# Another order of splits, copies and remainders around the last head pair of a hybrid encoder, with two token tiles' output products interleaved

## The reference

```python
def _dilated_attention_mixer(h, w_in, w_out):
    proj = h @ w_in                      # q, k, v of three dilation groups, and a gate
    for g, (window, dil) in enumerate(((128, 1), (512, 4), (2048, 16))):
        o, l = _dilated_group(q, k, v, window, dil, slopes)    # softmax attention, log denominators
    wts = jax.nn.softmax(jnp.stack(lses, axis=-1), axis=-1)
    o = jnp.einsum('bshg,bshgd->bshd', wts, jnp.stack(outs, axis=3))
    y = o.reshape(bsz, s, A_WIDTH) * jax.nn.silu(gate)
    return y @ w_out

x = _layer_norm(DEEPNORM_ALPHA * x + gate * y, ln_g, ln_b)
```

## Time and profile before

| | us |
|---|---|
| median of 3 runs | 1970.03 (1969.86 to 1972.2) |
| profiled execution | 1972.37 |
| its span, first to last instruction | 1970.6 |
| mean granted clock of TensorE | 0.993 |

### The profile page before, as it was taken

The page is one execution under the profiler, slowest core; times in us unless marked ns, Lnnn a source line. Parts: engine busy times, 40 slices in busy tenths (PEclk is TensorE's granted clock), DMA queues, the critical chain, the costliest instruction groups (busy, mean ns, idle before and its releaser), DMA issues.

```text
span 1970.6 us, 33735 instructions
## 1 busy us (share of the span) xinstructions
PE 1917.3 (97%) x12422; PEld 1532.3 (78%) x12422; DVE 1301.3 (66%) x2634; ACT 1047.3 (53%) x2578; POOL 1266.0 (64%) x841
## 2 busy tenths in 40 slices
PE   7999999999999999999998999899999999999998
PEld 4788887888888878888877777687787777777887
DVE  6547566475664756646666767887788697587553
ACT  5455555555555555554562354864765765774320
POOL 0566776967769677686762825565666575586572
PEclk8999999999999999999999999999999999999999
DMA  9112222322223222132245416455455455366531
GB/s 293 53 60 70 79 86 62 97 69 76 81 71 94 64 78 86 63 96 71 79 146 184 145 54 150 135 148 161 135 171 150 138 168 146 133 191 231 180 119 43
DMA packets 117987, 229.45 MB, mean 116 GB/s; under 512 B 23104, under 2 KB 56256, under 8 KB 117824
## 3 DMA queue, kind: packets, MB, share of 16 engines
q1 hardware_dynamic: 117824, 227.29, 37.2%
HBM read 199.39 MB, written 27.86 MB: 115 GB/s over the span
## 4 chain that ended last, share of the span: by engine, by line
PE 81%; DVE 8%; ACT 3%; issue 3%; POOL 2%; SPq 2%; DMA 1%; DVEq 0%; ACTq 0%; POOLq 0%
PE pp L693 18%; PE pp_s L2581 15%; PE pp L696 9%; PE po L693 7%; PE po L696 4%; PE tp L775 3%; PE po L845 3%; PE sp_ L763 3%; DVE stage_s L3261 2%; PE yo_p L2785 2%; PE pp_s L2785 2%; PE st_p L2598 1%; PE st_p L2785 1%; PE fill L2785 1%; DVE vv L3182 1%
## 5 line engine op out<-in xcount | busy, mean ns | idle before, releaser
L693 PE MATMUL pp<-h_forms_hi,w_f 128*128 128x512 f32 x788 | 317.0, 402 | 3.2 <-ACT w_f L1049 3.2
L693 PE MATMUL pp<-h_forms_lo,w_f 128*128 128x512 f32 x788 | 308.2, 391 | 0.0
L579 POOL TENSOR_TENSOR w_f<-w_raw,w_f 128x512 fp32r<-128x512 f32 x154 | 197.1, 1300 | 145.0 <-ACT w_f L1049 145.0
L2581 PE MATMUL pp_s<-h_hi,w_hi_s 128*128 128x512 f32 x624 | 269.6, 432 | 5.4 <-DVE stage_s L3261 2.7
L2581 PE MATMUL pp_s<-h_hi,w_lo_s 128*128 128x512 f32 x624 | 244.9, 392 | 0.0
L2581 PE MATMUL pp_s<-h_lo,w_hi_s 128*128 128x512 f32 x624 | 244.3, 391 | 0.0
L696 PE MATMUL pp<-h_forms_hi,w_f 128*128 128x512 f32 x788 | 212.8, 391 | 0.0
L1110 ACT ACTIVATE prob<-prob,mz 128x256 f32<-128x256 f32 (+2 forms) x384 | 163.1, 428 | 83.0 <-DVE mz L1399 82.6
L579 POOL TENSOR_TENSOR w_f<-w_f_raw,w_f 128x512 fp32r<-128x512 f32 x117 | 155.3, 1327 | 77.0 <-ACT w_f L1049 77.0
L693 PEld LDWEIGHTS pp<-h_forms_hi,w_f 128*128 128x128 f32 x788 | 148.4, 188 | 32.0 <-DVE temps L1464 3.6
L696 PEld LDWEIGHTS pp<-h_forms_hi,w_f 128*128 128x128 f32 x788 | 148.2, 188 | 32.2
(11 more groups left out here) (581 smaller groups left out, 4753.5 us busy)
## 6 DMA issues: line engine op xcount, KB each, us to landing
w_raw<-in_a_w SPq DMA_DIRECT2D x80, 512.0 KB, 3.3
rw<-cum_rows SPq DMA_DIRECT2D x32, 1024.0 KB, 6.2
w_raw_s<-in_b_w SPq DMA_DIRECT2D x40, 512.0 KB, 4.4
ew<-exp_rows SPq DMA_DIRECT2D x64, 256.0 KB, 7.0
v<-in_ada_w SPq DMA_DIRECT2D x48, 256.0 KB, 3.3
qk<-merge_rows SPq DMA_DIRECT2D x42, 256.0 KB, 4.2
yT_b<-trunk SPq DMA_DIRECT2D x32, 256.0 KB, 2.6
stage_s<-yT_b SPq DMA_DIRECT2D x14, 512.0 KB, 4.7
```

The costliest lines, as they stand in the source:

```text
L579: return nc.gpsimd.tensor_tensor(out, x, hi.bitcast(F32), ALU.subtract)
L693: nc.tensor.matmul(bank, w1[:, b], h[:, b], start=b == 0 and t == 0, stop=False)
L2581: last = nc.tensor.matmul(out, w[:, slot, k, :], of_h(h, k, half), start=(k == 0 and n == 0), stop=(k == KT - 1 and n == 2))
```

## The change

On GpSimd, in `middle_forms`, the difference B21 - B22 stands ahead of low part 3 instead of behind it, in every unit whose forms GpSimd makes.

On the matrix engine, in `last_pair`, tile 0's chunks 0 and 1 stand together ahead of the value transposes, and from chunk 3 of tile 0 on the seven chunks of tile 1 are interleaved with the rest of tile 0. The loop over the following tiles starts at 2 instead of 1.

On ScalarE, weight split 1 goes ahead of the first tile, y split 0 behind numerators 7, weight split 2 ahead of the other half of the second tile, and numerators 8 behind weight splits 5 to 7.

On VectorE, y remainder 0 goes behind the unit's last sum (it stood ahead of it), and y remainder 1 ahead of `weigh_next` (3, 4, 5).

```diff
@@ middle_forms, GpSimd
                     nc.gpsimd.tensor_tensor(raw_form(n, 3), B22, B12, ALU.subtract).then_inc(t_made, 1)
-                    low_part(n, 3, raw_form(n, 3))
                     pool.wait_ge(w_ready, FORMS * n + 2)
                     nc.gpsimd.tensor_tensor(B21, B21, B22, ALU.subtract).then_inc(p_step, 1)
+                    low_part(n, 3, raw_form(n, 3))
@@ last_pair, TensorE
                     pe.wait_ge(y_lo_done, 1)
-                    out_products(0, (0,))
+                    out_products(0, (0, 1))
                     new_v(j, 8)
-                    out_products(0, (1,))
+                    out_products(0, (2,))
                     n = T_AT[("s", 0)]
                     transpose_last_stats(NT * j + n, n % 2)
-                    out_products(0, (2,))
                     duo_values(j, DUOS - 1)
-                    out_products(0, (3, 4, 5, 6)).then_inc(part_done, 1)
+                    out_products(0, (3,))
+                    pe.wait_ge(s_free, UNITS * PAIRS + 2)
+                    pe.wait_ge(y_lo_done, 2)
+                    out_products(1, (0, 1))
+                    out_products(0, (4,))
+                    out_products(1, (2, 3))
+                    out_products(0, (5,))
+                    out_products(1, (4,))
+                    out_products(0, (6,)).then_inc(part_done, 1)
+                    out_products(1, (5, 6)).then_inc(part_done, 1)
-                for m in range(1, 4):
-
-                    if m == 1:
-                        pe.wait_ge(s_free, UNITS * PAIRS + 2)
-                    elif m == 2:
+                for m in range(2, 4):
+
+                    if m == 2:
@@ last pair, ScalarE
                 both(j, 8)
+                split_w_out(1)
                 first_tile(j, c, LAST_DUOS[2], 1)
-                split_y(0)
-                split_w_out(1)
                 second_tile(j, c, LAST_DUOS[2], 1)
                 numerators(j, 7)
+                split_y(0)
+                split_w_out(2)
                 second_tile(j, c, LAST_DUOS[2], 0)
-                split_w_out(2)
                 split_w_out(3)
                 split_w_out(4)
-                numerators(j, DUOS - 1)
                 split_y(1)
                 split_w_out(5)
                 split_w_out(6)
                 split_w_out(7)
+                numerators(j, DUOS - 1)
@@ last pair, VectorE
-                second_sums(c, lambda: y_rest(0))
+                second_sums(c)
+                y_rest(0)
                 last_duo(j, 8)
                 new_v(j, 8)
                 event(j, ("s", 0))
+                y_rest(1)
                 weigh_next(j, (3, 4, 5))
-                y_rest(1)
                 join_values(j, DUOS - 1)
```

## The result

| | before, us | changed, us |
|---|---|---|
| median | 1970.24 (1967.88 to 1972.2, 10 runs) | 1974.35 (1969.66 to 1977.57, 10 runs) |
| profiled execution | 1972.37, span 1970.6 | 1976.44, span 1974.6 |
| mean granted clock | 0.993 | 0.993 |

The changed kernel is slower: ratio 1.0022 [1.0015, 1.003], 4.1 us. Forecast were 1966.4 us and a range of 1962.9 to 1970.3, so the time lies outside the range and on the other side of no change.

A forecast was written before the change was run, and what follows sets the result against it. The prediction took only the last pair and output stage, where the matrix engine waits on ScalarE and GpSimd, to have anything to give. A gain of 4.2 less 0.6 made 3.6 us: 1970.03 - 3.6 = 1966.4 us, range 1962.9 to 1970.3.

The forecast's parts named there:

- Part one: GpSimd's difference ahead of low part 3, all 39 units: fills a 0.74 us pause, low part still in time, cost 0.
- plus 8 us: Upper bound on the cost of GpSimd's reorder in the pairs, taken from the case of a late low part 3.
- the slower rival: In the pairs, low part 3 comes late at fourteen tight units, 0.6 us each, 8.1 us together: 1974.5 us; chance 6%.
- a wait in the fourth product of the pairs: Sign that the forecast is wrong: the matrix engine waiting at that product; no size given.
- Part two: Start of the output products: y split 0 comes later, so they begin near 1031.45 instead of 1030.76, cost 0.7 us.
- Part three: Tiles 0 and 1: no stall, a wait of 0.2 us at most; tile 2 near 1053.2, matrix engine 7.0 us ahead.
- Part four: Last pair's merge waits for broadcast weight rows; tile 4 starts at 1081.4 after a new 2.7 us wait, gain 4.2 us.
- the broadcast is not the limit: Rival at the merge: rows land by 1063, so the whole 7.0 us arrives, less up to 0.2: 1963.2; chance 10%.
- Part five: From tile 4 to the end: gain carried, but VectorE's meetings with GpSimd fall otherwise, net loss 0.6 us.
- the clock rival: Clock falls after a new wait, before tile 0 or tile 4: 1.7 us a fall, 1968.1 or 1969.8; chance 25%.

The follow-up runs named there:

- e10: Kernel before with GpSimd's new order alone, its difference also waiting for ScalarE's rounding of form 3, so the pause stays: 1970.61 us, ratio 1.0004.
- e12: e4 with y split 0, y remainder 0 and weight split 1 back at their old places: 1964.12 us, ratio 0.9971 to before.
- e4: e2 with the last pair's differences and shares ahead of y remainder 2 and y split 2: 1965.86 us, ratio 0.9975 to before.
- e6: Kernel before with only the last pair's differences and shares moved ahead of y remainder 2 and y split 2: 1969.80 us, ratio 0.9998.
- e2: Changed kernel with GpSimd's old order restored, so the last pair's new order alone: 1967.24 us, ratio 0.9989 to before.
- e1: Kernel before with only GpSimd's difference B21 - B22 moved ahead of low part 3: 1976.83 us, ratio 1.0037.
- e11: Kernel before with GpSimd's new order in 32 of 39 units, all but the seven made while a pair begins: 1970.19 us, ratio 1.0002.
- e3: e1 with VectorE's small sums (shares) moved behind the first bank's copy and the second bank's sum: 1970.68 us, ratio 1.0002 to before.
- e7: Changed kernel, GpSimd's new order kept, with the shares moved as in e3 and the table's last steps as in e4: 1966.92 us, ratio 0.9979 to before.

## Why the prediction was wrong, by its own steps

**Part one, cost 0: this step failed, and it alone turned the sign.** It walked through all 39 units, but with one question, whether the low part is in time for the matrix engine. It is (e10). The other question was not put: what had happened in the 0.74 us of GpSimd's pause that now was filled. The row of the pause was cited the earlier trace rows, the rule of the lock was cited, the 1.09 against 2.11 us was cited the earlier trace rows; the three were not brought together at VectorE's only two-operand sums that stand ahead of a bank's copy. The bound "plus 8 us" was the right size by luck, from a wrong mechanism: the slower rival put the delay into the low part, priced it at 8.1 us and gave it 6%. Measured: 6.9 by the medians and 7.4 in the trace, by seven late copies. Among the signs of being wrong stood "a wait in the fourth product of the pairs", and the seven waits are just there; but the prediction expected it of low part 3, which would show at line 696, and not of the bank's copy, at line 693. Where VectorE stood beside GpSimd I had used the old durations of its small sums, as if they were its own; 0.21 was the duration of a sum in a pause.

**Part two, +0.7 us: right in its place.** Tile 0's products began at 1035.74; less the 4.29 that the changed kernel was behind by then, 1031.45, as forecast (before: 1030.76). One wait of 2.3 became 1.45 and 1.29. That it reaches the end was not shown (e12).

**Part three, no stall in tiles 0 and 1: right.** GpSimd's last remainders ended in time, the 4.7 us wait is gone. Tile 2 was forecast near 1053.2. It began at 1059.95; less 4.29 and the 2.7 of the clock at tile 0 that is 1053.0.

**Part four, the broadcast is next: right in mechanism.** VectorE's row before the merge in the changed kernel:

```profile
1074.24 1.90 DVE L1799 TENSOR_TENSOR h_tail<-h_tail,num 128x512 f32<-128x512 f32 x3 [4.49 <-DMA h_tail<-merge_rows]
```

The landing is last, as said, and the wait ahead of tile 4 is 2.46, forecast 2.7. Tile 4 began at 1088.47; less 4.29 and 2.7 it is 1081.5, forecast 1081.4. The prediction's rival "the broadcast is not the limit" is out. e4 and e6 confirm the two chains: the earlier landing is worth something in the new order (e4) and nothing in the old (e6).

**Part five, -0.6, and the clock rival: here a term was mis-sized.** The remainder 6 took 1.78 us, not 2.11, and tile 4 took 11.40 instead of 9.53. The rival with a 25% chance and 1.7 us a fall was right at tile 4 each time. The sum of the tail with it is 4.2 - 0.6 - 1.9 = 1.7; e2 measured 2.7, with an interval (0.4 to 3.7 us by the ratio) that holds this and can't tell more. The fall at tile 0 is in no such sum: three of six traces with the old last pair have it too, which one trace of before could not tell. But it costs about 1 us there and 2.7 to 2.9 in the new order, so a part of it belongs to the change and stood in no term but the rival's.

**The frame.** That the two traces differ by 4.0 us of span and the medians by 4.1 is partly chance. Between the traces: -3.1 at the start, +7.4 in the pairs, -0.3 behind them, where the changed one had the fall at tile 0 and before's had not, and before's had the fall at 1138 us and the changed one had none. Between the medians, by e1 and e2: +6.9 and -2.7. The start is chance as far as can be told: the eight traces with the new last pair all begin early (63.21 or less at the early product), of the other six only e11, but the median of a kernel less the two later stretches of its trace is 64.5 us on average over the eight and 64.6 over the six, an estimate from the two tables. The range ended at 1970.3 because everything above it was left to the one slower rival at 6%. The upper bound of 8 us in part one should have weighed more, since a step that is made 39 times was priced from the one consumer that I had looked at.

## What to carry to other kernels

Before filling an engine's pause, look at what the other engines did in it: list every VectorE instruction with two SBUF operands that overlaps the pause, and follow who stands behind it in VectorE's order. A small instruction's duration in a trace may be that of a free lock, and beside a busy GpSimd it is one GpSimd instruction more. Keeping the pause cost nothing (e10), and so did an order that fills no pause beside such sums (e11); moving the sums behind the copy that others wait for took away the waits on it, but in two traces 2.0 and 3.6 us of 7.4 remained (e3, e7). And when a stall is removed, look for the second chain that ends within a few us, since each of the two edits alone (e2 in part, e6 wholly) brings less than both.

## What the runs showed of the hardware

- Sums of 32 by 64 elements took 0.21 us in a pause of GpSimd's and 1.19 to 1.22 us beside a busy one, in the changed kernel at every one of seven places, while a reciprocal of the same shape (0.54) and a copy out of PSUM (0.67) were not held.
- The same instructions in the same order found the clock at 1.00 in some executions and at 0.5 to 0.8 in others behind a wait of 1.3 to 2.3 us at tile 0; behind 2.4 to 2.5 us ahead of tile 4 it fell in four traces out of four, and behind 2.4 us ahead of layer B's first product in seven out of fourteen. "TensorE: Matmul & The Clock Gate" of the Trainium skill, section "What's actually happening", has half rate as the default that activity lifts; the rows agree, but no run here shows what decides between the executions.
- The same early product came at 60.88 to 65.94 us in fourteen traces, by the granted clock from 40 to 60 us: at 1.00 in 60.9 to 61.1, at 0.91 in 62.6 to 63.2, at 0.83 in 64.5 to 64.8, at 0.74 in 65.7 and 65.9. That is as much as the change's tail is worth; two traces are best laid over each other behind it.
